# Another order of the on-chip tensors in a two-block transformer kernel

## The reference

```python
h = rms_norm(x, norm_pre[i])
(aq, ak, av, az, dq, dk, dv, db, da, dz, gate_att, gate_dn) = split_cols(h @ w_in[i])
y_att = (gqa_attention(q, k, v) * silu(az)) @ w_br_att[i]
qkv = silu(short_conv(concatenate([dq, dk, dv]), conv_w[i]))          # 5 taps per channel
y_dn = (rms_norm(bidir_gated_deltanet(qd, kd, vd, g, beta)) * silu(dz)) @ w_br_dn[i]
x = x + rms_norm((sigmoid(gate_att) * y_att + sigmoid(gate_dn) * y_dn) @ w_out[i])
x = x + rms_norm(sigmoid(x @ w_ple_gate[i]) * (p[i] @ w_ple_proj[i]))
for i in range(2):                                                     # second block
    x = x + mixer_i(rms_norm_2(x, attn_norm[i]))                       # stick-breaking, then differential
    x = x + (silu(n @ w_gate[i]) * (n @ w_up[i])) @ w_down[i]          # n = rms_norm_2(x, ffn_norm[i])
```

## Time and profile before

| | |
|---|---|
| median of three runs | 2242.45 us (2241.71 to 2244.97) |
| the profiled execution | 2241.71 us, span 2239.9 us |
| TensorE busy | 2169.0 us, 97% |
| VectorE busy | 1200.0 us, 54% |
| ScalarE busy | 1009.1 us, 45% |
| GpSimd busy | 253.2 us, 11% |
| moved by DMA | 185.77 MB, mean 83 GB/s |

### The profile page before, as it was taken

The page is one execution under the profiler, slowest core; times in us unless marked ns, Lnnn a source line. Parts: engine busy times, 40 slices in busy tenths (PEclk is TensorE's granted clock), DMA queues, the critical chain, the costliest instruction groups (busy, mean ns, idle before and its releaser), DMA issues.

```text
span 2239.9 us, 35310 instructions
## 1 busy us (share of the span) xinstructions
PE 2169.0 (97%) x14886; PEld 1685.0 (75%) x14886; DVE 1200.0 (54%) x2101; ACT 1009.1 (45%) x1919; POOL 253.2 (11%) x273
## 2 busy tenths in 40 slices
PE   6999999999999999899999999999999999999999
PEld 4777777777777887676666888888777777888887
DVE  5576666666744556533334643444566665443442
ACT  4565655656655236544444432223455544222231
POOL 0023121221220011122122000000100001000000
PEclk9999999999999999999999999999999999999999
DMA  4222221212224342111111223223211112222222
GB/s 173 76 81 77 67 64 62 86 67 72 72 74 145 118 145 81 57 57 50 45 43 71 99 94 100 89 95 109 79 57 40 55 61 90 94 95 93 97 101 85
DMA packets 34765, 185.77 MB, mean 83 GB/s; under 512 B 4000, under 2 KB 4384, under 8 KB 15408
## 3 DMA queue, kind: packets, MB, share of 16 engines
q1 hardware_dynamic: 34608, 183.53, 24.0%
HBM read 172.99 MB, written 7.90 MB: 81 GB/s over the span
## 4 chain that ended last, share of the span: by engine, by line
PE 89%; DVE 6%; ACT 2%; issue 2%; DMA 0%; POOL 0%; POOLq 0%; SPq 0%; DVEq 0%; ACTq 0%
PE ps L1585 88%; PE ps L1588 1%; DVE spl L2025 1%; ACT arena L2477 1%; DVE arena L2175 0%; DVE x L2354 0%; ACT hh L2477 0%; ACT arena L2480 0%; ACT spl L2480 0%; DVE hl L2322 0%; DMA x<-xT 0%; DVE arena L2169 0%; DVE arena L2214 0%; DVE x L2318 0%; DVE x L2302 0%
## 5 line engine op out<-in xcount | busy, mean ns | idle before, releaser
L1585 PE MATMUL ps<-hh,spl 128*128 128x512 f32 x3120 | 1033.1, 404 | 23.9 <-DVE hl L2322 5.7
L1585 PEld LDWEIGHTS ps<-hh,spl 128*128 128x128 f32 x3120 | 584.9, 189 | 175.9 <-issue 42.1
L1585 PE MATMUL ps<-hl,spl 128*128 128x512 f32 x1552 | 628.5, 405 | 0.0
L2025 DVE TENSOR_TENSOR spl<-raw,spl 128x512 fp32r<-128x512 f32 x596 | 416.9, 725 | 169.7 <-ACT spl L2480 169.1
L1585 PE MATMUL ps<-arena_r,spl 128*128 128x512 f32 x1936 | 458.1, 391 | 8.7 <-DVE x L2354 8.7
L1585 PEld LDWEIGHTS ps<-arena_r,spl 128*128 128x128 f32 x1936 | 362.5, 188 | 89.4 <-DVE x L2354 12.1
L2480 ACT ACTIVATE spl<-raw 128x512 fp32r<-128x512 f32 x596 | 342.2, 618 | 137.9 <-PE ps L1585 137.1
L1585 PEld LDWEIGHTS ps<-hl,spl 128*128 128x128 f32 x1552 | 293.5, 189 | 68.2 <-issue 12.3
L1585 PE MATMUL ps<-arena 32*32 32x32 f32 (+6 forms) x5664 | 216.8, 224 | 12.1 <-DVE arena L2214 5.8
L2477 ACT ACTIVATE arena<-arena 128x512 f32<-128x512 f32 (+2 forms) x211 | 139.7, 663 | 183.9 <-DVE arena L2359 141.2
L1585 PEld LDWEIGHTS ps<-arena 32*32 32x32 f32 (+4 forms) x5664 | 125.9, 116 | 96.8 <-issue 73.9
(11 more groups left out here) (232 smaller groups left out, 1963.4 us busy)
## 6 DMA issues: line engine op xcount, KB each, us to landing
raw<-wstream SPq DMA_DIRECT2D x149, 1024.0 KB, 5.0
arena<-spill SPq DMA_DIRECT2D x17, 256.0 KB, 5.5
GS<-g_rows SPq DMA_DIRECT2D x16, 256.0 KB, 3.3
spill<-x SPq DMA_DIRECT2D x14, 256.0 KB, 2.8
arena<-arena SPq DMA_DIRECT2D x20, 128.0 KB, 2.7
x<-xT SPq DMA_DIRECT2D x4, 512.0 KB, 7.6
spill<-arena SPq DMA_DIRECT2D x8, 256.0 KB, 2.1
x<-xT SPq DMA_DIRECT2D x1, 2048.0 KB, 7.4
```

Source lines behind the costliest of these rows:

```text
L1585: return pe.matmul(out, lhsT, rhs, start=start, stop=stop, skip_group_check=True)
L2025: tt(spl[:, p % 2, 1, c], raw[:, p % 2, c], spl[:, p % 2, 0, c].bitcast(F32), ALU.subtract) \
```

## The change

The declarations at the top of `build` stand in another order. No length, type or name changes, and neither does any instruction: each engine issues the same instructions with the same waits in the same order, and only the start addresses of the operands differ. `raw`, `spl`, `x`, `hh` and `hl` keep their places; the other tensors get new ones.

```diff
@@ build
         hl = sb("hl", [128, KT, S], F32R)
+        cst = sb("cst", [128, len(CONST_NAMES), 128])
+        vec = sb("vec", [128, NVEC])
+        with nc.sbuf_tensor("pad", [128, 2, S], F32) as pad:
+            pass
+        pad_r = sb("pad_r", [128, 2, S], F32R)
+        small = sb("small", [128, 600])
+        with nc.sbuf_tensor("GS", [128, 2, S], F32) as GS:
+            pass
+        GS_r = sb("GS_r", [128, 2, S], F32R)
+        ident_r = sb("ident_r", [128, 128], F32R)
+        mask_r = sb("mask_r", [128, 130], F32R)
         NA = 41
         with nc.sbuf_tensor("arena", [128, NA, S], F32) as arena:
             pass
         arena_r = sb("arena_r", [128, NA, S], F32R)
-        with nc.sbuf_tensor("pad", [128, 2, S], F32) as pad:
-            pass
-        pad_r = sb("pad_r", [128, 2, S], F32R)
-        with nc.sbuf_tensor("GS", [128, 2, S], F32) as GS:
-            pass
-        GS_r = sb("GS_r", [128, 2, S], F32R)
         with nc.sbuf_tensor("on_t", [128, 2, S], F32) as on_t:
             pass
         on_r = sb("on_r", [128, 2, S], F32R)
+        st = sb("st", [128, 2, 2, 128])
+        kdt = sb("kdt", [128, 2, 128])
         with nc.sbuf_tensor("rv", [128, 2, 2, 128], F32) as rv:
             pass
         rv_r = sb("rv_r", [128, S], F32R)
-        st = sb("st", [128, 2, 2, 128])
-        kdt = sb("kdt", [128, 2, 128])
-        cst = sb("cst", [128, len(CONST_NAMES), 128])
-        ident_r = sb("ident_r", [128, 128], F32R)
-        mask_r = sb("mask_r", [128, 130], F32R)
-        vec = sb("vec", [128, NVEC])
-        small = sb("small", [128, 600])
```

## The result

The changed kernel takes 2255.72 us (median of 4 runs, 2254.97 to 2256.79); the kernel before, run beside it, 2243.11 us (4 runs, 2241.71 to 2244.97). The ratio is 1.0056, with a 95% interval of 1.0041 to 1.0072: slower by 12.6 us. The forecast was 2242.4 us with a range of 2237 to 2250, so it is wrong. Rival A gave 2256.7 us.

A forecast was written before the change was run, and what follows sets the result against it. The prediction took TensorE to bound the kernel, busy 97% of the span and 89% of the chain. To the profiled 2241.71 us it added 0 for every term, then took the runs' median: 2242.4 us, range 2237 to 2250.

The forecast's parts named there:

- Rival A: TensorE pays per 64-byte line: 7.1 ns on each of 2016 matmuls, 14.3 us slower, 2256.7 us; chance 6%.
- Part 2, TensorE: Phase within 64 bytes for TensorE's moving rows: taken as 0 us from the gate's small transposes, upper end left open.
- a count of 121 would be rival A: Sign in the profile after: 121 arena_r matmuls per 28 us instead of 125 would mean TensorE pays per 64-byte line.
- Part 1: Place of a tensor in its partition, all engines: 0 ns per instruction, under 0.3 us at the bounds.
- Rivals B and C: TensorE clock after idle stretches: one more fall, 2247.5 us, 4%; or the falls go away, 2233.9 us, 4%.
- Rival D: Engines collide less, VectorE's L2025 loses its 40 ns surplus: 2239.7 us; 5% for more than 4.5 us.

The follow-up runs named there:

- e9: Kernel before with 32 unused bytes ahead of raw, so every tensor moves by 32 bytes and distances stay: 2243.44 us, ratio 1.0002.
- e3: Kernel before with 32 unused bytes ahead of hh, so hh, hl and everything behind move by 32 bytes while spl stays: 2272.28 us, ratio 1.0132.
- e4: Kernel before with spl moved by 32 bytes and hh, hl, arena and the rest by 64: 2273.13 us, ratio 1.0135.
- e13: Kernel before with spl moved by 32 bytes, hh and hl by 256, arena by 288, the rest by 512: 2260.98 us, ratio 1.0085.
- e10: Kernel before with hh and hl moved by 128 bytes, arena and what follows by 256, spl unmoved: 2259.57 us, ratio 1.0075.
- e8: Kernel before with 128 unused bytes ahead of raw, so all tensors move by 128 bytes: 2242.41 us, ratio 0.9999.
- e1: Changed kernel with 32 unused bytes ahead of arena, putting arena back on a multiple of 256 from spl: 2242.77 us, beside 2243.23 for the kernel before.
- e2: Kernel before with 32 unused bytes ahead of arena and 32 behind it, old order kept: 2254.95 us, ratio 1.0049.
- e5: Kernel before with 64 unused bytes ahead of arena and 64 behind it: 2246.65 us, ratio 1.0013.
- e11: Kernel before with hh and hl moved by 96 bytes, arena and what follows by 192, spl unmoved: 2273.02 us, ratio 1.0137.
- e14: Kernel before with hh and hl moved by 160 bytes and arena used from 264 bytes further on: 2274.55 us, ratio 1.0143.

## Why the prediction was wrong

**The step that failed** is "Part 2, TensorE": "I take 0, the value of the nearest row". What the runs showed in its place: 6.3 ns for each of the 1936 matmuls out of arena_r, 12.2 of the 12.6 us.

The nearest rows were the gate's transposes, 272 ns for an operand off a multiple of 64 and for one on it. They say nothing of a 512-column row, for three reasons. The operand that was off is not the moving one. In a transpose the data is loaded as weights, and the moving row is the identity in cst, on a multiple of 64:

```profile
L1588 PEld LDWEIGHTS ps<-cst,small x4: 88/90/90, 60.9 to 61.4; 128*16 128x16 f32 x4
```

The 272 ns are recorded durations, and those hardly tell columns apart: matmuls of 8 columns in the same stage take 256.

```profile
L1585 PE MATMUL ps<-small,cst x18: 254/256/303, 57.7 to 59.6; 128*128 128x8 f32 x16, 128*128 128x64 f32 x2
```

And in steps, worked out from the starts as above, a column of these f32 matmuls takes about twice as long as one in fp32r: 109 ns for 128 columns and 429 ns for 512 out of pad, 0.84 ns each, against 227 / 512 = 0.44 ns. That leaves time in which a small hindrance of the reads could hide. The changed kernel has the like: for transposes out of arena, whose start is now 224 past a multiple of 256 from cst, both the duration and the step (109 ns) stay.

```profile
L1588 PE MATMUL ps<-cst,arena x124: 270/272/331, 80.6 to 1845.8; 128*128 128x128 f32 x124
```

A row where an engine may have time to spare can't bound one where it has none. The prediction saw that ("the upper end stays open") and still left the open end 6% and outside the range. With no row between 0 and 14.3 us for 2016 matmuls of the engine that carries 89% of the chain, the range had to reach to A's 2256.7.

**Rival A** had the right place, the right sign and nearly the right size: 7.1 ns foretold, 6.3 measured, 14.3 us against 12.6. Its cause is refuted. The number of 64-byte lines that a moving row touches is the same in e9 as in e3, and e9 pays nothing; in e4 and e13 moving rows that touch no line too many pay all of it. The near hit is chance. The sign "a count of 121 would be rival A" came as 122, which could not tell the two causes apart, since both are a longer step.

**The question was framed too narrowly.** The prediction laid out each address modulo 64 and asked for each tensor alone: "does the place in a partition matter, and does the phase within 64 bytes matter?" Every operand's row was asked for, the pair never: that weights are loaded during the matmul (PEld is busy 75% of the span) stood in the first row read. Part 1 compared hh, arena_r and rv_r and found them equal, and took it that the place costs nothing; all three lay at distance 0 from spl, so it was one place measured three times. In e10, where hh keeps its phase within 64 bytes and moves by 128, it costs 4.6 ns per step.

**The address within a partition.** The start of a tensor moves TensorE's step from 226.6 to 232.9 ns (arena_r, before and after); e8 and e9 show that only the distance counts, and e1, e10 and e13 that a multiple of 256 bytes is free. The Trainium skill, SBUF — State Buffer, section "Door 1: The DMA port swizzle", was read by the prediction for its banks of four partitions and its 16-byte lines, and 0 us was worked out from both for a shift by 32 bytes. The traces of this case disagree with that estimate for TensorE: e2 and e5 shift arena by whole 16-byte lines and are 11.7 and 3.4 us slower. The measurement decides.

**Two rows misread, without weight in the sum.** The 145.01 us are not the chain's longest piece; the ones of 361.93 and 355.50 us are longer. And the 28 us from 1288 us do not lie before arena_r is read at all (that is from 707.9 us on the earlier trace rows); they are merely out of hh and hl alone.

**What held.** VectorE, in spite of new phases: L2131 has medians of 743 to 745 ns (744 to 746 before), L2366 692 as before.

```profile
L2366 DVE TENSOR_TENSOR arena<-arena x44: 691/692/693, 1248.2 to 2188.4; 128x512 f32<-128x512 f32 x44
...
L2131 DVE SCALAR_TENSOR_TENSOR arena<-pad,vec,arena x16: 708/743/1300, 64.9 to 444.8; 128x510 f32<-128x510 f32 x8, 128x511 f32<-128x511 f32 x8
```

DMA: landings within 0.1 us of the earlier trace rows, and GpSimd's wait for the rotated copies 118.0 us against 119.1.

```profile
arena<-arena SPq DMA_DIRECT2D x20, 128.0 KB, 2.8
...
on_t<-spill SPq DMA_DIRECT2D x5, 256.0 KB, 2.9
...
vec<-vecs SPq DMA_DIRECT2D x1, 235.5 KB, 2.6
```

```profile
POOL arena L2867 <- DMA arena<-arena: 118.0, 7, 40.0
```

ScalarE is busy 1009.1 us in both. Rivals B and C: the fall of the clock at 903 us is there again, in the other order:

```profile
903.00:910.00 7.00, 3.00 (x5) 0.60 (x3) 0.74 (x2) 3.80 (x6) 0.00 (x0) 0.74 0.29 123
910.00:917.00 7.00, 3.37 (x7) 2.08 (x8) 6.86 (x11) 3.77 (x7) 0.00 (x0) 0.53 0.01 2
```

(0.26 + 0.47) x 7 = 5.1 us lost, as before; the stretches from 168 and from 224 us are at 0.97 again. Rival D: L2025 has a mean of 729 ns against 725, so no collisions went away:

```profile
L2025 DVE TENSOR_TENSOR spl<-raw,spl 128x512 fp32r<-128x512 f32 x596 | 419.4, 729 | 170.8 <-ACT spl L2480 170.1
```

**What stays open.** That the distance between the moving row and the weights in spl decides is shown by e3, e4, e9 and e13, and that no other engine or DMA takes part by the steps with all of them silent. Which part of TensorE or of the memory makes it matter was not tried. That it is the load of the next weights reading beside the moving row is argued and not shown: no run takes the load away. Nor is it known why 64 bytes cost so little (1.8 ns) and 4 bytes so much (10.5 ns), or why so many steps ahead of 694 us are longer than 229 ns in the kernel before.

## What to carry to other kernels

Where TensorE runs fp32r matmuls of 512 columns without pauses, as here, the moving operand and the weights loaded beside it should start at equal addresses modulo 256 bytes; 32 bytes of filling in the wrong place cost this kernel 0.5% to 1.35%. For the two kinds of matmul in the next section that does not hold. To look for it, count full-width matmuls per fixed stretch for each pair of tiles, and shift one tensor, then all together: a loss with one and none with all is a distance. When equal rows are used as evidence that an address is free, first work out in what respect the addresses differ at all.

## What the runs showed of the hardware

Of the matmuls in this kernel only those in fp32r with 512 columns pay. (The views print f32 for both; raw float32 are those out of pad, on_t and others with weights in cst, while hh, hl, spl and the names with `_r` are fp32r.) Those with f32 operands keep their 592 ns and their step of 429 ns in the changed kernel, though pad and on_t moved to 96 and 224 past a multiple of 256 from their weights in cst (both at 0 before):

```profile
L1585 PE MATMUL ps<-pad,cst x48: 590/592/667, 76.5 to 1812.8; 128*128 128x512 f32 x48
L1585 PE MATMUL ps<-on_t,cst x32: 590/592/697, 213.0 to 1851.2; 128*128 128x512 f32 x32
```

The 256-column matmuls, with the moving row in spl and the weights in hh or hl, go the other way: off distance 0 they are slightly faster. Before and in e3:

```profile
L1585 PE MATMUL ps<-spl,hh x576: 274/283/682, 34.4 to 1813.4; 128*128 128x256 f32 x192
```

```profile
L1586 PE MATMUL ps<-spl,hh x576: 277/281/683, 34.9 to 1833.8; 128*128 128x256 f32 x192
```

Their step goes from 119.2 to 117.7 ns (117.5 in e11, 116.6 in e13; in e10 and e14 it is 118.1 to 119.1), and there are 864 of them, so it is worth at most about 2 us of the kernel. I have no reason for it.
